# A root moved three steps later in the attention loop, and the head normalisation moved ahead of the maxima

## The reference, cut to what matters

```python
s = jnp.einsum("bqhmd,bkhmd->bhmqk", qblk, k).astype(f32) * scale   # m: two score maps per head
p = jax.nn.softmax(jnp.where(causal, s, -1e30), axis=-1)
w = p[:, :, 0] - lam * p[:, :, 1]
o = jnp.einsum("bhqk,bkhe->bqhe", w.astype(v.dtype), v)
...
o = rms_norm(o, head_gain) * (1.0 - lam_init)                        # over the 128 features of a head
```

## Time and profile before

| | us |
|---|---|
| median of 3 runs | 1184.45 (1184.27 to 1186.23) |
| the profiled execution's own time | 1185.46 |
| its span | 1183.7 |
| PE busy | 1154.8 (98%) |
| DVE busy | 647.6 (55%) |
| ACT busy | 398.2 (34%) |
| mean granted TensorE clock | 0.994 of full speed |

### The profile page before, as it was taken

One profiled execution on the slowest core, in us unless ns is written; L12 is line 12 of the kernel. 1 busy time (PEld: TensorE's weight loads), 2 busy tenths in 40 slices (PEclk: granted clock), 3 DMA queues, 4 the chain that ended last, 5 costly groups with the idle time before them and its releaser, 6 DMA issues.

```text
span 1183.7 us, 13613 instructions
## 1 busy us (share of the span) xinstructions
PE 1154.8 (98%) x5236; PEld 933.8 (79%) x5236; DVE 647.6 (55%) x857; ACT 398.2 (34%) x670; POOL 34.6 (3%) x47
## 2 busy tenths in 40 slices
PE   7999999999889999999999999999999999999997
PEld 6888887777556788788888888888888888888886
DVE  6666755755586557744544444443544444444458
ACT  7433823554546346622122122112112112112122
POOL 0300000000020100200000000000000000000000
PEclk9999999999989999999999999999999999999999
DMA  6111323112000452021011111111111111101112
GB/s 225 52 36 53 125 89 89 36 37 54 19 34 7 163 177 101 19 89 54 20 70 54 37 52 53 47 41 53 53 35 53 53 35 53 53 35 60 48 54 107
DMA packets 21094, 74.74 MB, mean 63 GB/s; under 512 B 2832, under 2 KB 2960, under 8 KB 20928
## 3 DMA queue, kind: packets, MB, share of 16 engines
q1 hardware_dynamic: 17568, 63.45, 15.6%
q10 hardware_dynamic: 1824, 4.29, 1.6%
q0 software_dynamic: 1664, 6.49, 1.6%
HBM read 65.82 MB, written 4.19 MB: 59 GB/s over the span
## 4 chain that ended last, share of the span: by engine, by line
PE 93%; DVE 4%; DMA 1%; ACT 1%; issue 1%; ACTq 0%; SPq 0%; DVEq 0%
PE pair L309 28%; PE pair L311 28%; PE pair L310 28%; PE pair L621 3%; PE pair L656 2%; PE pair L638 1%; DMA raw<-weights 1%; PE pair L624 1%; DVE negmax L1456 1%; PE pair L470 1%; DVE diag L1477 0%; DVE wl L1280 0%; PE pair L667 0%; SPq L394 0%; PE pair L727 0%
## 5 line engine op out<-in xcount | busy, mean ns | idle before, releaser
L1676 DVE TENSOR_TENSOR yacc<-yacc,pair 128x1024 f32<-128x1024 f32 x112 | 136.7, 1220 | 133.0 <-PE pair L311 133.0
L309 PE MATMUL pair<-yh,wh 128*128 128x512 f32 x512 | 199.7, 390 | 1.6 <-DVE yl L1603 0.9
L310 PE MATMUL pair<-yl,wh 128*128 128x512 f32 x512 | 199.4, 389 | 0.0
L311 PE MATMUL pair<-yh,wl 128*128 128x512 f32 x512 | 199.4, 389 | 0.0
L310 PE MATMUL pair<-wdl,xh 128*128 128x512 f32 x480 | 187.1, 390 | 0.0
L309 PE MATMUL pair<-wdh,xh 128*128 128x512 f32 x480 | 187.1, 390 | 0.0
L311 PE MATMUL pair<-wdh,xl 128*128 128x512 f32 x480 | 186.9, 389 | 0.0
L1664 DVE TENSOR_TENSOR relu<-relu 128x512 f32<-128x512 f32 x64 | 44.3, 692 | 213.4 <-ACT xh L1212 213.4
L898 ACT ACTIVATE wdh<-raw 128x1024 fp32r<-128x1024 f32 x30 | 30.3, 1055 | 278.6 <-PE pair L311 274.4
L1280 DVE TENSOR_TENSOR wl<-raw,wh 128x1024 fp32r<-128x1024 f32 x70 | 87.1, 1245 | 59.1 <-ACT wh L898 58.4
L1209 ACT ACTIVATE relu<-pair 128x512 f32<-128x512 f32 x64 | 38.3, 598 | 228.5 <-PE pair L311 228.5
(11 more groups left out here) (212 smaller groups left out, 1462.1 us busy)
## 6 DMA issues: line engine op xcount, KB each, us to landing
raw<-weights SPq DMA_DIRECT2D x104, 512.0 KB, 3.3
x_sb<-x SPq DMA_DIRECT2D x8, 512.0 KB, 7.7
q_rot<-q_sb ACTq DMA_DIRECT2D x32, 128.0 KB, 2.4
out<-h_sb SPq DMA_DIRECT2D x7, 512.0 KB, 2.6
x_a<-x POOLq DMA_DIRECT2D x4, 512.0 KB, 7.1
x_b<-x POOLq DMA_DIRECT2D x4, 512.0 KB, 6.7
cos_t<-rope POOLq DMA_DIRECT2D x1, 1024.0 KB, 5.1
gw_raw<-gate_weights POOLq DMA_DIRECT2D x1, 512.0 KB, 3.7
```

The source lines that it names most:

```text
L309: pe.matmul(o, a_hi, b_hi, start=first, stop=False)
L310: pe.matmul(o, a_hi, b_lo, start=False, stop=False)
L311: return pe.matmul(o, a_lo, b_hi, start=False, stop=last)
L1676: dve.tensor_tensor(y, y, pair[2 + t % 2][:, :], ALU.add).then_inc(y_added, 1)
```

## The change

`head_roots(0)` goes from step 21 to step 24 on ACT. On DVE, `head_rstd(0)` and the diagonals of head 0 go from step 24 to 25 and those of head 1 from 25 to 26. The four spreads on PE and the scaling of the four half heads on DVE go from steps 25 to 28 to steps 26 to 29. The scaling also goes from the end of its step to the place between the combination and the maxima (in step 26, where the maxima come first, behind the combination). The rounded copies go from steps 28 and 30 to 29 and 31, their low parts from 29 and 31 to 30 and 32. `head_vars(0)` stays at step 21, and `lru_mix` and the weight pieces stay where they are. No instruction is added or taken away.

```diff
@@ -323,11 +323,11 @@
         lru_mix = [22, 24, 26, 28]
-        head_mix = [28, 30]
+        head_mix = [29, 31]

         EARLY_NORM = 2 * TT
-        spread_at = [25, 26, 27, 28]
+        spread_at = [26, 27, 28, 29]
@@ -1084,7 +1084,7 @@
-                if s == EARLY_NORM + 5:
+                if s == EARLY_NORM + 8:
                     head_roots(0)
@@ -1478,16 +1478,8 @@
-            def early_norm(s):
-
-                if s == EARLY_NORM + 5:
-                    head_vars(0)
-                if s == EARLY_NORM + 8:
-                    dve.wait_ge(qk_bank, UNITS)
-                    head_rstd(0)
-                    diagonals(0)
-                if s == EARLY_NORM + 9:
-                    diagonals(1)
+            def spread_norm(s):
+
                 if s in spread_at:
                     n = spread_at.index(s)
                     h, hf = divmod(n, 2)
@@ -1495,6 +1487,17 @@
                     dve.wait_ge(spread_done, n + 1)
                     dve.scalar_tensor_tensor(q, q, head_gain[:, 0:1], bank(4), ALU.mult,
                                              ALU.mult).then_inc(o_norm_half, 1)
+
+            def early_norm(s):
+
+                if s == EARLY_NORM + 5:
+                    head_vars(0)
+                if s == EARLY_NORM + 9:
+                    dve.wait_ge(qk_bank, UNITS)
+                    head_rstd(0)
+                    diagonals(0)
+                if s == EARLY_NORM + 10:
+                    diagonals(1)
@@ -1509,6 +1512,7 @@
                 if 1 <= s <= steps:
                     combine_step(s - 1)
+                spread_norm(s)
                 if s < steps and not max_first:
                     max_step(s)
```

## The result

The changed kernel takes 1187.57 us in the median of 22 runs (1185.9 to 1193.4), the kernel before 1185.99 in 22 runs (1184.27 to 1188.01) on the same chip. The ratio is 1.002 with an interval of 1.0012 to 1.0028: slower, by 1.6 us by the medians and 2.4 by the ratio, as by the means (1188.16 against 1185.75). The forecast was 1183.6, between 1181.2 and 1186.2, so it is wrong in direction and in range. Five of the 22 runs of the changed kernel take over 1190 (mean granted clock 0.986 to 0.990), and none of the kernel before over 1188.01; without these five the means are 1.4 apart.

A forecast was written before the change was run, and what follows sets the result against it. PE was taken to bound the kernel, with 93% of the chain. Terms -2.8 - 1.8 + 1.6 + 4.7 - 3.6 = -1.9 us, off the profiled 1185.46, gave 1183.6 us, range 1181.2 to 1186.2.

The forecast's parts named there:

- Point 1: Steps 21 to 23: root leaves step 21, PE stands 2.1 us instead of 4.9 before step 23's scores: -2.8 us.
- Point 2: Step 23: clock stays up after the shorter wait, scores take 2.98 us instead of 4.77: -1.8 us.
- Point 3: Steps 24 to 26: root arrives in step 24, POOL stretches head 0's diagonals to 3.75 us: +1.6 us.
- the rival of the clock falling at the new wait: Step 26: clock falls as PE stands 3.3 us before the first spread: +4.0 us, 1187.6 us; chance 0.1.
- Points 4 and 5: Steps 27 to 29, scaling ahead of maxima: +4.7 us; weight cast and low part clear of POOL: -3.6 us.
- the weight cast that it clears: Step 27: weight piece no longer takes 3.03 us, clear of POOL's third operation: -1.8 us.
- the later low part: Head 0's low part, moved from step 29 to 30, clears POOL's fourth operation, 1.22 us instead of 2.97: -1.8 us.
- Point 6: Steps 31 and 32: head 1's rounded copy and low part cost nothing; about 1 us if their cover failed.
- the rival in which POOL meets a combination: Step 26: POOL's third operation comes first and delays the combination by up to 2.35 us: 1185.9 us; chance 0.08.

The follow-up runs named there:

- twelfth experiment: Changed kernel with only its root moved to step 23 instead of 24: 1184.04 us against 1185.79 for the kernel before, ratio 0.999.
- sixth experiment: Kernel before with five matmuls of unread result added before the scores of step 23: 1184.88 us, ratio 0.9998 to the kernel before.
- first experiment: Changed kernel with the four scalings put back behind the maxima: 1184.2 us against 1185.68 for the kernel before, ratio 0.9989.
- fourth experiment: Kernel before with only the rounded copies moved to steps 29 and 31, low parts to 30 and 32: 1184.96 us, ratio 0.9991.
- third experiment: Kernel before with only the scalings moved between combination and maxima, in their old steps 25 to 28: 1191.15 us, ratio 1.0046.
- fifth: Changed kernel with unread matmuls added, two before step 23's scores and three before the first spread: 1186.78 us, ratio 1.001 to the kernel before.
- seventh experiment: Changed kernel with the recurrence's second copy on ACT in step 23 instead of 24: 1184.94 us, ratio 0.9991 to the kernel before.
- eleventh experiment: Kernel before with only the recurrence's second copy moved to step 23: 1185.2 us, ratio 0.9997 to the kernel before.

## Why the prediction was wrong

**Point 1 holds.** No table load stands between the weight cast (319.32) and the exponentials (320.28), and PE stands 1.98 instead of 4.94 before the scores of step 23. Forecast was 2.1. This wait differs between executions: with the root in step 21 it is 4.08 to 4.94 in the five traces that have nothing added there, without it 1.13 to 2.18 in six.

**Point 2 failed.** The clock was to stay up after a wait of 2.1. It falls: the scores take 3.93, with a clock of 0.57 from 323 to 331. The lead at step 24 is 3.8, not 4.6: 3.0 from the shorter wait and 0.8 from the clock, where the point had 1.8. The reason given, that the new wait is nearer to the harmless ones of up to 1.1, does not carry: the clock also fell at 194 in this execution, where PE's only wait of the 5 us before was 1.16 long. Nor does the length of the wait decide by itself, for in the twelfth experiment the scores of step 23 start after 2.02 us of standing and take 2.97. The price of 1.8 was right: from step 23 to 24 that execution takes 8.20 us, 1.8 under the 10.01 of before. But its clock falls at 330 instead, and steps 24 and 25 take 9.28 us, 1.5 more than in the changed kernel. So what the point had wrong is that the slow stretch can be removed at this wait; the sixth experiment shows the same in the old order.

**Point 3 was right in its parts and short in its sum.** The root waits for, the copy behind it, POOL on the diagonals, 3.80 us of them, PE standing 2.99 (forecast 3.3): each came as walked through. From step 24 to the first spread the change lost 0.1 more than forecast. But from the spread to the scores of step 27 are 347.65 - 342.66 = 5.0 us, where the forecast had 3.5, and 1.1 of the difference is the products at the lower clock. That is the rival of the clock falling at the new wait, which had a chance of 0.1. Its place and its cause were right, its price of 4.0 was too high for this place (1.5), and its chance far too low. What it said against itself, that the wait is a third shorter than the one that did it, was the same unfounded threshold as in point 2. The two are one assumption, and the forecast had counted on it twice as if it were two. A passage that the prediction did not use speaks against it: the Trainium skill (TensorE: Matmul & The Clock Gate, A second HAM failure mode: psum-queue depth-cycling) tells of a kernel whose short idle times between groups of matmuls make the clock go up and down. The trace here agrees, with three falls in one execution, at 194, 323 and 344.

**Points 4 and 5 in sum.** From step 27 to 31 the forecast was +1.1 (4.7 - 3.6), the trace has +2.0. The order, less the weight cast that it clears, was 4.7 - 1.8 = 2.9; measured 3.0 between the steps of the first experiment and the changed kernel, and 3.7 by the ratios. The mis-sized term is the later low part: -1.8 was the whole stall of that cast, the fourth experiment shows -1.0. (The 4.7 is three times 1.6, which is 4.8; the slip is small.) The range of +2.2 to +5.5 for the order did hold it in the changed kernel; the third experiment, +5.5, is its upper end.

**The sum.** 0.8 (clock, point 2), 1.6 (step 26, nearly all clock) and 0.9 (low part) are 3.3 us, and turn -1.9 into the +1.35 of the loop. By the ratio it is +2.4. The difference from the trace may be that in the new order some executions have a fall in steps 28 to 30 as well, which costs 2.3 and 2.5 in the fifth and seventh experiment, and the profiled execution had none there; the five runs above 1190 with clocks of 0.990 and less fit this, but none of them has a trace. Point 6 cost nothing that a trace shows.

**What else was assumed.** The median of the three runs shown, 1184.45, was low: in 22 runs it is 1185.99. The forecast's time of 1183.6 was reckoned from the profiled execution, 1185.46, and is not touched by this; its range and chances were read against 1184.45. The Trainium skill's longer table load (ScalarE: Activation LUTs, What ACT_TABLE_LOAD costs) is again not seen: in step 24 load, root and copy start at 336.27, 337.57 and 337.69.

## What to carry to other kernels

Before an operation is moved, list what its new step already holds: here a table switch, a POOL operation and a wait of PE's met in one step, and moving either of two small things by one step was worth 3.5 us. The original aim, the wait in step 21, paid only when the root did not arrive in that full step: nothing with the root in step 24, 3.2 us with it in step 23. A small normalising operation belongs behind the maxima, not between an engine's result and the exponentials that the next matmuls wait for; ahead of them it cost 3.0 us, and falls of the clock beside it another 2.3 to 2.5. And where PE stands every few microseconds, price the lower clock as something that comes in some place of the stage, not as the work of one long wait that can be removed: all fourteen traces here have at least one fall between 320 and 338.

## What the runs showed of the hardware

- The granted clock falls from 2.4 to 1.2 GHz in this stage after waits as short as 1.16, 1.83 and 1.98 us, at places that differ between executions and kernels (321, 329, 344, 353, 357), and in other executions the same waits of 1.16 (191.59 in the kernel before) and 1.83 us (358.09 in the changed kernel) and one of 2.02 us (twelfth experiment) have no fall behind them. What decides it stays open.
- What a fall costs depends on its place. From the scores of step 23 to those of step 24 are 7.7 to 8.2 us at full clock and 9.2 to 10.2 with a fall; from step 24 to 26 7.8 to 8.0 and 9.3 to 9.9 (the eleventh experiment, where POOL holds DVE up, aside); from step 27 to 31, with the scaling ahead of the maxima, 22.0 and 24.3 to 24.5.
- DVE and POOL hold each other up both ways. POOL's operation at 327.85 took 3.26 instead of 2.35 where DVE's combination had begun 0.24 ahead of it, and the combination kept its 1.28 (seventh experiment); the rival in which POOL meets a combination had it the other way round, and a DVE operation of 16 columns took 1.66 instead of 0.17 (eleventh). The Trainium skill (SBUF — State Buffer, Who interferes with whom) says that issue order decides who blocks; both rows agree.
- The load of the exponentials' table comes directly ahead of the next exponential and not behind the root: at 338.75, with the recurrence's copy (337.69, 1.04) between them and no load before it.
